# The opening of a fused two-model stack: x also read transposed, fewer and larger first weight transfers, and the retention norm factor applied behind its products

## The reference

```python
def rmsnorm(x, g):
    y = x * lax.rsqrt(jnp.mean(x * x, axis=-1, keepdims=True) + 1e-6)
    return y * g

h = rmsnorm(x, norm_mix_pre[0])                 # 256 x 1024
proj = h @ ret_w_in                             # 1024 -> 6144: q, k, v, g of 4 heads
q, k = apply_rotary(q, ...), apply_rotary(k * 256 ** -0.5, ...)   # 256 wide a head
scores = (q @ k.T) * decay                      # causal, gamma ** (n - m)
y = scores @ v                                  # 512 wide a head (written in chunks)
mu, var = mean(y), mean((y - mu) ** 2)          # over the 512
yn = (y - mu) * lax.rsqrt(var + 1e-6) * gn_gain
out = (silu(g) * yn) @ ret_w_out
x = x + rmsnorm(out, norm_mix_post[0])
```

## Time and profile before

| | before |
|---|---|
| median of 3 runs | 1244.16 us (1244.06 to 1244.37) |
| span of the profiled execution, first to last instruction | 1242.4 us |
| TensorE busy in the span | 1230.6 us (99%) |
| VectorE / ScalarE / GpSimd busy | 807.9 / 695.0 / 144.4 us |
| DMA | 208.54 MB, 168 GB/s over the span |
| DMA in the first fortieth (31 us) | 332 GB/s |
| mean granted clock of TensorE | 0.999 |

### The profile page before, as it was taken

The page is one execution under the profiler, slowest core; times in us unless marked ns, Lnnn a source line. Parts: engine busy times, 40 slices in busy tenths (PEclk is TensorE's granted clock), DMA queues, the critical chain, the costliest instruction groups (busy, mean ns, idle before and its releaser), DMA issues.

```text
span 1242.4 us, 19229 instructions
## 1 busy us (share of the span) xinstructions
PE 1230.6 (99%) x7514; PEld 1105.9 (89%) x7514; DVE 807.9 (65%) x1231; ACT 695.0 (56%) x1002; POOL 144.4 (12%) x178
## 2 busy tenths in 40 slices
PE   9999999999999999999999999999999999999997
PEld 8888888888888999999998888888999899999896
DVE  5666656767667566666666878677666666666564
ACT  6444345655555655555554766555576556566554
POOL 1000001200001000000000410430201410201500
PEclk9999999999999999999999999999999999999999
DMA  8544443755554644444443655545454453363331
GB/s 332 207 164 169 170 157 134 255 186 190 189 185 144 199 157 134 147 142 140 152 167 130 224 201 182 200 157 183 148 175 164 143 200 106 117 205 138 136 136 51
DMA packets 33846, 208.54 MB, mean 168 GB/s; under 512 B 3985, under 2 KB 4258, under 8 KB 16226
## 3 DMA queue, kind: packets, MB, share of 16 engines
q1 hardware_dynamic: 31986, 201.32, 46.9%
q0 software_dynamic: 1488, 5.78, 1.3%
q10 hardware_dynamic: 288, 0.27, 0.1%
HBM read 206.30 MB, written 1.05 MB: 167 GB/s over the span
## 4 chain that ended last, share of the span: by engine, by line
PE 94%; DVE 3%; ACT 2%; issue 1%; POOL 0%; DVEq 0%; ACTq 0%; POOLq 0%
PE pair L600 18%; PE pair L602 17%; PE pair L601 17%; PE pair L742 12%; PE pair L736 6%; PE bank L600 3%; PE bank L602 3%; PE bank L601 3%; PE bank L1037 1%; PE bank L1062 1%; PE bank L1045 1%; PE bank L855 1%; ACT whi L1484 1%; PE bank L1012 1%; DVE wlo L2013 1%
## 5 line engine op out<-in xcount | busy, mean ns | idle before, releaser
L2013 DVE TENSOR_TENSOR wlo<-raw,whi 128x2048 fp32r<-128x2048 f32 (+5 forms) x208 | 431.2, 2077 | 216.1 <-ACT whi L1484 215.3
L1484 ACT ACTIVATE whi<-raw 128x2048 fp32r<-128x2048 f32 (+5 forms) x208 | 361.7, 1742 | 184.1 <-PE pair L602 156.1
L600 PE MATMUL pair<-whi,bhi 128*128 128x384 f32 (+3 forms) x528 | 189.3, 359 | 1.9 <-DVE blo L2039 1.6
L602 PE MATMUL pair<-whi,blo 128*128 128x384 f32 (+3 forms) x528 | 183.7, 348 | 0.0
L601 PE MATMUL pair<-wlo,bhi 128*128 128x384 f32 (+3 forms) x528 | 183.7, 348 | 0.0
L600 PE MATMUL pair<-whi,ahl 128*128 128x384 f32 (+3 forms) x416 | 153.5, 369 | 0.8 <-DVE wlo L2013 0.8
L742 PE MATMUL pair<-ahl,whi 128*128 128x512 f32 x640 | 153.2, 391 | 0.0
L601 PE MATMUL pair<-wlo,ahl 128*128 128x384 f32 (+3 forms) x416 | 149.1, 358 | 0.0
L602 PE MATMUL pair<-whi,ahl 128*128 128x384 f32 (+3 forms) x416 | 149.1, 358 | 0.0
L742 PEld LDWEIGHTS pair<-ahl,whi 128*128 128x128 f32 x640 | 117.5, 188 | 22.6
L600 PEld LDWEIGHTS pair<-whi,bhi 128*128 128x128 f32 x528 | 100.9, 191 | 11.7 <-issue 2.9
(11 more groups left out here) (322 smaller groups left out, 1879.0 us busy)
## 6 DMA issues: line engine op xcount, KB each, us to landing
raw<-wstream_d SPq DMA_DIRECT2D x136, 1024.0 KB, 4.9
raw<-wstream_d SPq DMA_DIRECT2D x56, 768.0 KB, 4.2
raw<-wstream_d SPq DMA_DIRECT2D x4, 832.0 KB, 4.4
raw<-wstream_d SPq DMA_DIRECT2D x4, 800.0 KB, 4.8
gain_row<-rows_d POOLq DMA_DIRECT2D x5, 512.0 KB, 4.2
arena<-mem_d POOLq DMA_DIRECT2D x2, 1024.0 KB, 7.1
raw<-wstream_d SPq DMA_DIRECT2D x4, 384.0 KB, 3.2
raw<-wstream_d SPq DMA_DIRECT2D x4, 288.0 KB, 2.8
```

The lines of the kernel that those rows point to most:

```text
L600: pe.matmul(out_ap, lhi, rhi, start=first, stop=False, skip_group_check=True)
L602: return pe.matmul(out_ap, llo, rhi, start=False, stop=last, skip_group_check=True)
L1484: act.activation(whi[:, n % RING, 0:width[n]], raw[:, n % RAW, 0:width[n]], ACT.Copy).then_inc(hi_ready, 1)
L2013: dve.tensor_tensor(wlo[:, n % RING, 0:width[n]], raw[:, n % RAW, 0:width[n]], whi[:, n % RING, 0:width[n]].bitcast(F32), ALU.subtract).th ...
```

## The change

x is passed a second time, transposed on the host into `x_cols` (8 column tiles of 128 features by 256 tokens). ScalarE's queue loads it in two transfers of 512 KB, and ScalarE and VectorE make `ahi` and `alo` from it in SBUF. The transposes of x, the 8 fillers and one of the 12 warm-up products go. The rows of x, needed for the squares and for the residual, come after chunk 3. Chunk 0 is loaded in two transfers in place of four and chunk 1 in one in place of two; they are still split in parts, and chunk 2 is now split in two parts also. The cos and sin table is stored once, read twice through a broadcast view, and loaded apart from the decay table. ident comes after the decay table.

The factor of the norm is no longer in the cos and sin table. The scores' instruction multiplies by the key's factor as well as by the decay. The query's factor is left out, because the group norm divides it away: GpSimd adds eps times (mean square + eps) of the token to the variance in place of eps. v and g are read out as before.

```diff
-FIRST_PARTS = ((0, 512, 1024, 1536, CW), (0, 1024, CW))
-WARM_UP = 12
+FIRST_PARTS = ((0, 512, 1024, 1536, CW), (0, 1024, CW), (0, 1024, CW))
+FIRST_LOADS = ((0, 1024, CW), (0, CW), (0, CW))
+WARM_UP = 11
...
-    ret = np.concatenate(decay + [cos, cos, sin, sin], axis=1)
+    ret = np.concatenate(decay + [cos, sin], axis=1)
...
-        rcos, rsin = tables[:, 1024:1536], tables[:, 1536:2048]
+        rcos, rsin = (tables[:, at:at + SEQ].unsqueeze(1).to_broadcast([P, 2, SEQ]) for at in (1024, 1024 + SEQ))
+        x_cols = cut(10000, KD, SEQ)
...
         def _(sp):
-            sp.dma_start(ident[:, :], ident_d).then_inc(ident_in, 16)
-            for t in range(NT):
-                sp.dma_start(x[:, t, :], x_in[t * P:(t + 1) * P, :]).then_inc(x_in_sem[t], 16)
             n = 0
-            for c, cuts in enumerate(FIRST_PARTS):
+            for c, cuts in enumerate(FIRST_LOADS):
...
-            for c in range(len(FIRST_PARTS), RAW):
-                load(c)
+            decays = RET_HEADS * SEQ
+            sp.dma_start(tables[:, decays:decays + 2 * SEQ], ret_in[:, decays:]).then_inc(turning_in, 16)
+            load(RAW)
+            for t in range(NT):
+                sp.dma_start(x[:, t, :], x_in[t * P:(t + 1) * P, :]).then_inc(x_in_sem[t], 16)
+            load(RAW + 1)
+            sp.dma_start(tables[:, 0:decays], ret_in[:, 0:decays]).then_inc(ret_tables_in, 16)
+            sp.dma_start(ident[:, :], ident_d).then_inc(ident_in, 16)
+            load(RAW + 2)
             sp.dma_start(cols[:, DEPTH * KD:], cols_d[:, DEPTH * KD:]).then_inc(cols_in_sem, 16)
-            sp.dma_start(tables[:, :], ret_in).then_inc(ret_tables_in, 16)
...
+            def group_rsqrt():
+                pool.wait_ge(var_ready, w.up("var"))
+                pool.tensor_tensor(var_eps[:, 0:NT], sq_sum[:, 0:NT], ffn_eps, ALU.add).then_inc(rstd_step, 1)
+                inverse_root(rstd[:, 0:NT], NT, rstd_ready, "rstd")
+
-            x_rsqrt()
+            raw_rsqrt(EPS)
             load_gain(0)
             for _ in range(RET_HEADS):
-                rsqrt(var_ready, w.up("var"), sq_sum[:, 0:NT], rstd[:, 0:NT], 1.0)
+                group_rsqrt()
...
                             pe.wait_ge(part_hi, 1)
-                            pe.wait_ge(turned_hi, 1)
+                            pe.wait_ge(x_hi, 1)
...
-            pe.wait_ge(ident_in, 16)
-
-            ready = turn_rows(loaded)
-            keep_warm(pair[:, 1, 0, 0:P], 8)
+
+            def cols_ready(a, b):
+                pe.wait_ge(x_lo, (b + 1) // 2)
...
-                features("v", ahi, alo, lhs_ready=ready, between=() if h else [nothing, nothing, nothing, spread_rows])
+                features("v", ahi, alo, lhs_ready=None if h else cols_ready)
...
             act.dma_start(cols[:, 0:DEPTH * KD], cols_d[:, 0:DEPTH * KD]).then_inc(mix_gain_in, 16)
+            for g in range(2):
+                act.dma_start(x_cols[:, 4 * g:4 * g + 4, :], x_cols_in[:, 4 * g:4 * g + 4, :]).then_inc(x_cols_sem[g], 16)
...
             def first_rows(g):
-                turn_out([(ahi, 0)], (2 * g, 2 * g + 1), [COLS["norm_mix_pre"]], bank[:, g, :])
+                act.wait_ge(x_cols_sem[g // 2], 16)
+                for k in (2 * g, 2 * g + 1):
+                    at = COLS["norm_mix_pre"] + k
+                    ins = act.activation(ahi[:, k, :], x_cols[:, k, :], ACT.Copy, scale=cols[:, at:at + 1])
+                ins.then_inc(x_hi, 1)
...
-            split_hi(-1)
-            row_squares(lambda t: act.wait_ge(x_in_sem[t], 16))
+            first_hi(2, 0)
+            first_hi(2, 1)
...
                 if h == 0:
-                    x_scale_ready()
+                    row_squares(lambda t: act.wait_ge(x_in_sem[t], 16))
...
                 if h == 0:
-                    spread_row()
+                    x_scale_ready()
...
             def first_rows(g):
-                turn_out([(ahi, alo, 0)], (2 * g, 2 * g + 1), [COLS["norm_mix_pre"]], bank[:, g, :])
+                dve.wait_ge(x_hi, g + 1)
+                for k in (2 * g, 2 * g + 1):
+                    ins = low_half(alo[:, k, :], x_cols[:, k, :], ahi[:, k, :], COLS["norm_mix_pre"] + k)
+                ins.then_inc(x_lo, 1)
...
-                dve.tensor_tensor(r_sc[:, 0:SEQ], bank[:, 0, 0:SEQ], decay[:, h, :], ALU.mult).then_inc(masked, 1)
-                dve.tensor_tensor(r_sc[:, SEQ:384], bank[:, 0, SEQ:384], decay[:, h, 0:P], ALU.mult).then_inc(masked, 1)
+                for kt, (at, n) in enumerate(((0, SEQ), (SEQ, P))):
+                    dve.scalar_tensor_tensor(r_sc[:, at:at + n], bank[:, 0, at:at + n], x_rstd[:, kt:kt + 1], decay[:, h, 0:n],
+                                             ALU.mult, ALU.mult).then_inc(masked, 1)
...
-                    turning = tables[:, 1024:2048].rearrange("p (a s) -> p a s", a=4)
-                    dve.wait_ge(spread_out, w.up("spread"))
-                    step(dve.tensor_tensor(turning, turning, rstd_row[:, :].unsqueeze(1).to_broadcast([P, 4, SEQ]), ALU.mult))
+                    dve.wait_ge(turning_in, 16)
```

More of the change, by code:

```diff
@@ L181, in shape_tables, with hybrid_stack @@
     return ident, np.ascontiguousarray(ret), np.ascontiguousarray(dil), np.ascontiguousarray(sec)
-def hybrid_stack(nc, x_in, wstream, cols_d, rows_in, gate_in, mem_in, pos_in, ident_d, ret_in, dil_in, sec_in, out):
+def hybrid_stack(nc, x_in, x_cols_in, wstream, cols_d, rows_in, gate_in, mem_in, pos_in, ident_d, ret_in, dil_in, sec_in, out):
     chunks, starts, _ = chunk_plan()
@@ L316, in hybrid_stack @@
         x_in_sem = [sem(f"x_in{t}") for t in range(NT)]
+        x_cols_sem = [sem(f"x_cols_in{g}") for g in range(2)]
+        x_hi, x_lo = sem("x_hi"), sem("x_lo")
+        turning_in = sem("turning_in")
         ident_in, mix_gain_in, cols_in_sem, seeded = sem("ident_in"), sem("mix_gain_in"), sem("cols_in"), sem("seeded")
-        part_in = [sem(f"part_in{i}") for i in range(sum(len(ps) - 1 for ps in FIRST_PARTS))]
+        part_in = [sem(f"part_in{i}") for i in range(sum(len(ps) - 2 for ps in FIRST_LOADS))]
         part_hi, part_lo = sem("part_hi"), sem("part_lo")
@@ L544, in _ @@
             load_gain(3)
-            ffn_rsqrt()
+            raw_rsqrt(D * EPS)
             pool.wait_ge(max_ready, ATT_HEADS)
@@ L652, in tokens @@
                     c = w.chunk
-                    pe.wait_ge(lo_ready, c + 1)
+                    if c >= len(FIRST_PARTS):
+                        pe.wait_ge(lo_ready, c + 1)
                     slot = c % RING
                     for s in range(len(ks)):
+                        if c < len(FIRST_PARTS) and s * wd in FIRST_PARTS[c]:
+                            pe.wait_ge(part_lo, part_count(c, s * wd))
                         if lhs_ready is not None and s % 2 == 0:
@@ L951, in ret_turn @@
             def ret_turn(h):
+                if h == 0:
+                    pe.wait_ge(ident_in, 16)
                 pe.wait_ge(z_ready, h + 1)
@@ L969, in _ @@
                     ret_turn(h - 1)
+            w.up("x_rstd", NT)
             second_free = []
@@ L1469, in first_hi @@
                 a, b = FIRST_PARTS[c][i:i + 2]
-                act.wait_ge(w_landed[c] if b == CW else part_in[part_count(c, a) - 1], 16)
+                act.wait_ge(part_in[0] if c == 0 and b <= FIRST_LOADS[0][1] else w_landed[c], 16)
                 ins = act.activation(whi[:, c, a:b], raw[:, c, a:b], ACT.Copy)
@@ L2157, in _ @@
             first_lo(1, 1)
-            split_lo(-1)
+            first_lo(2, 0)
+            first_lo(2, 1)
             def rotate(h):
@@ L2165, in rotate @@
                 for b in range(2):
-                    dve.tensor_tensor(r_c[:, b, :], pair[:, p, b, :], rcos, ALU.mult).then_inc(dve_step, 1)
-                    ins = dve.tensor_tensor(r_s[:, b, :], pair[:, p, b, :], rsin, ALU.mult)
+                    halves = lambda rows: rows.rearrange("p (a s) -> p a s", a=2)
+                    dve.tensor_tensor(halves(r_c[:, b, :]), halves(pair[:, p, b, :]), rcos, ALU.mult).then_inc(dve_step, 1)
+                    ins = dve.tensor_tensor(halves(r_s[:, b, :]), halves(pair[:, p, b, :]), rsin, ALU.mult)
                     ins.then_inc(dve_step if b == 0 else drained_v[p], 1)
@@ L2178, in ret_decay @@
                     dve.wait_ge(mixed, h)
-                dve.tensor_tensor(r_sc[:, 0:SEQ], bank[:, 0, 0:SEQ], decay[:, h, :], ALU.mult).then_inc(masked, 1)
-                dve.tensor_tensor(r_sc[:, SEQ:384], bank[:, 0, SEQ:384], decay[:, h, 0:P], ALU.mult).then_inc(masked, 1)
+                else:
+                    dve.wait_ge(ret_tables_in, 16)
+                    dve.wait_ge(x_rstd_ready, NT)
+                for kt, (at, n) in enumerate(((0, SEQ), (SEQ, P))):
+                    dve.scalar_tensor_tensor(r_sc[:, at:at + n], bank[:, 0, at:at + n], x_rstd[:, kt:kt + 1], decay[:, h, 0:n],
+                                             ALU.mult, ALU.mult).then_inc(masked, 1)
             def ret_norm(h, g_at):
@@ L2747 @@
```

(2 more changed lines are left out.)

14 lines of the change are left out of this document (5 added, 9 removed).

## The result

The changed kernel takes 1246.29 us in the median of 21 runs (1245.58 to 1247.0), the kernel before 1244.10 (1243.45 to 1245.24, 21 runs): a ratio of 1.0017, 95% interval 1.0011 to 1.0023. The span of its profiled execution is 1244.7 us against 1242.4. The loss is about 0.2%, small but clear of the noise, where 2 us of gain were forecast, and it lies outside the range given.

The account below looks back on a forecast made before the run. TensorE was taken to bound the kernel. An earlier first product (1.53) plus part 2 (0.44) took 1.97 us off the span, 1242.4 to 1240.4; with 1.8 carried over, 1242.2 us, range 1241.0 to 1244.7.

Parts of the forecast that it names:

- What bounds the kernel: Whole kernel: TensorE carries 94% of the chain that ended last, so its next product's possible start is what counts.
- First product = data at hand + 1.41: Opening: ScalarE's two scaled copies and weight copy put TensorE's first product 1.41 us after the columns land.
- Columns at 6.4 us: Opening: the first 512 KB of columns land at 6.4 us, first product at 7.85, a gain of 1.5.
- My upper bound: Column landing: at most 6.2 us from issue, the weight quarters' median; landing 7.35, product 8.8, gain 0.6.
- the case of one queue starving: Rival on column loading: SP's 3 MB of weights go first, columns land at 10.3 to 11.3 us; chance 0.05.
- The clock: Rival at the first products: idle TensorE starts at 1.2 GHz, loss 0.9 to 2.5, time 1243.1 to 1244.7; chance 0.26.
- part 2: Norm factor moved behind the products: no spread products, 0.44 us gained on TensorE; later group norm step costs 0.
- VectorE's chain of 7.0 us: First block: VectorE's work from ScalarE's first scaled columns to chunk 1's first half stays 7.0 us; TensorE's 0.3 wait stays.
- Part 3: Rows, tables and ident loaded later: cost 0, all cover 2 us or more.
- The sum: Whole kernel: 1.53 + 0.44 = 1.97 us off the span, time 1242.2, 0.16% less.
- 'slower': Rival: SP's queue served first, product at 11.8 to 12.8 us, time 1246.1 to 1247.1; chance 0.05.

Follow-up runs that it names:

- columns in time: Variants of the changed kernel with the gains, or both column transfers, moved to SP's queue: 1243.28 to 1244.71 us.
- 18 warm-ups: Changed kernel with 18 warm-up products and all on SP's queue: columns 0 to 3, chunk 0's halves, columns 4 to 7, chunk 1; 1243.28 us.
- part 2 alone: The kernel before with only the norm's factor applied behind the products (also called the norm factor alone): 1243.48 us, 0.9994 of before.
- columns and weights in the second order: Changed kernel, 11 warm-up products, all on SP's queue: columns 0 to 3, chunk 0's halves, columns 4 to 7, chunk 1; 1243.84 us.

## Why the prediction was wrong, point by point

- **What bounds the kernel**: right. What the change gained and lost can be read from when TensorE's next product starts.
- **First product = data at hand + 1.41**: right for the columns (8.90 to 10.38 is 1.48). It left out a second condition, the weights. They set the first product in every variant with the columns in time and a 512 KB first piece (weights used at 7.2 to 8.1 us, product 0.7 later). The changed kernel hid this, because its columns came later still.
- **Columns at 6.4 us**: this step failed first. It measured 8.9, and the product 10.38 instead of 7.85. I counted bytes and let the two queues share them evenly, and I took the 8 KB ahead of the columns as nothing. The runs show turns, in which tiny packets count like large ones: taking those 128 tiny packets off the queue is worth 3.5 us of landing, doubling them costs 1.7 (3.1 and 1.2 without what the issue itself takes). My upper bound, 6.2 us from issue to landing, came from a queue with no other large one beside it, and from its smallest transfers: the two of 512 KB in the same view took 7.6. I gave the case of one queue starving a chance of 0.05, and reasoned only of 3 MB ahead, not of packets.
- **The clock**: named as a rival at 0.26, priced at 0.9 to 2.5; it happened, for 1.4 (13.95 against 12.99 us from the first product to the second block's second, with the 0.44 of part 2 taken off). It was priced for an idle time of 2 us; with the columns late it became 4.8. The sum put this term at nothing, though late columns lengthen the very gap that lowers the clock. With 11 warm-ups and an idle of 2.8 to 3.0 us (columns in time) the clock was low too; after 0.9 us (the norm factor alone, the coarser loads alone) it was high. A gap of 2 us, as forecast, is in no run. Nor is the rise a fixed moment: I read it at 6.9 us from one profile, and the spacing of the warm-up products puts it anywhere from 3.8 to 7.1 in the others.
  The Trainium skill (TensorE: Matmul & The Clock Gate, Part 1) has half rate as the default that activity lifts; the traces agree, at 0.50 after the idle time and 1.00 near 15.2.
- **VectorE's chain of 7.0 us**: right in this kernel, though it held TensorE nowhere, because the half clock made TensorE later still. Where the columns come early the chain is longer, as it then waits for weights (8.2 us with 18 warm-ups). In this kernel it runs from 9.84 to the first half of chunk 1, done near 16.8, as the rows show:

```profile
9.84 0.88 DVE L2060 SCALAR_TENSOR_TENSOR ahl<-arena,cols,ahl 128x256 fp32r<-128x256 f32 x2 [9.84 <-ACT ahl L1587]
...
15.60 2.36 DVE L2161 TENSOR_TENSOR wlo<-raw,whi 128x1024 fp32r<-128x1024 f32 x2
```

- **Part 2, 0.44**: right; 0.50 in the profile of that part alone, 0.63 by the medians, whose interval reaches across no change. The group norm's sum, feared to take 0.70, took 0.19, as GpSimd's timeline at the last head has it against the earlier trace rows:

```profile
178.72 0.19 POOL L538 TENSOR_TENSOR stat<-stat 128x2 f32<-128x2 f32 x1 [25.61 <-DVE stat L2221]
178.99 0.69 POOL L491 TENSOR_TENSOR stat<-stat 128x2 f32<-128x2 f32 x1
```

- **Part 3, hidden**: right. TensorE has no wait between 20 and 40 us. The coarser loads are hidden too in this kernel. Alone they make the first product 0.4 us later, of which 0.2 is left at the second block.
- **The sum**: forecast -1.97. In the profiles: landing +1.0, clock with the vanished wait +1.4, part 2 -0.44, together +1.96, and 0.3 more near 702 us, where VectorE's subtraction of a whole chunk took 2.61 us instead of 2.29. That 0.3 is in the profiles of the changed kernel and of all nine variants of it, and in none of the kernel before, part 2 alone and the coarser loads alone. In the changed kernel this subtraction (from 704.31) runs beside a GpSimd step for 0.46 us, before (from 702.29) for 0.11. Whether that is the cause, and what shifted the two, stays open.
- **Rivals**: 'slower' was there, and the measured 1246.29 lies within its price (1246.1 to 1247.1), but that is coincidence: it had the columns landing at 10.3 or later, where they landed at 8.8 and the clock made up the rest. No rival had both a late landing and the half clock.

## What to carry to other kernels

Here two DMA queues shared the engines packet by packet, so what a transfer cost beside a busy queue went with its number of packets and the size of the other's, not with its bytes. Put tiny-packet transfers where no large ones run beside them, or behind the transfer that is waited for. And before taking filler work from TensorE in an opening, look at what sets the first product twice, for each operand, and count what the idle time does to the clock.

## What the runs showed of the hardware that was not expected

- 128 packets of 64 bytes landed 5.4 us after their issue beside a queue of 4 KB packets (4.3 to 4.9 in the variants), 2.0 us in the kernel before, where the other queue began with packets of 512 bytes. They held the transfer behind them by 3.1 us, a second such set by 1.2. Beside packets of 8 KB, as many of 4 KB went (104 and 99 from 7 to 10 us).
  The Trainium skill (DMA: Bandwidth & Descriptors, Queues, rings and completion order) says that each DMA engine goes round its rings and drains a group of some 9 to 17 descriptors from one before it turns to the next. An estimate by that page: an engine's 8 descriptors of gains wait out one turn of the other ring, 9 to 17 of 4 KB, 1.5 to 2.8 us at a sixteenth of 400 GB/s. The runs agree in size (1.2 us for the second such transfer, 3.1 for the first) and with the going round, but not with the groups: 102 of the 128 packets started right behind a large one, so most turns were of one packet. The prediction didn't weigh this rule, and it would have spoken against the change.
- The DMA engines move only 227 to 279 GB/s between 3 and 6 us at 0.9 busy, and over 420 from 7 us on, in the variant with columns and weights on one queue; before, it was 360 to 381 from 3 to 5 us and 150 between 6 and 7. With the columns in time, the first 512 KB of weights were usable at 7.2 to 8.1 us and not sooner.
- TensorE's clock rises at different moments for the same work. The warm-up products are 0.21 us apart at first and then 0.11, and that change comes at 3.8 us (columns and weights in the second order), 5.0 (the changed kernel), 6.3 (28 warm-ups), 6.9 (the transposes of the kernel before) and 7.1 (18 warm-ups). The granted clock reads 1.00 all the while, so until the first fall the spacing has to be read and not the row.
- In the changed kernel TensorE idled from 5.6 us; the row falls to 0.50 between 8 and 9 and is back near 15.2, 4.8 us into the products. With the gains on SP's queue it fell only near 9.3, half a microsecond after the first product. With the idle time filled (28 warm-ups) it did not fall.
